# An expert's weight tile read as one run of 8192 bytes a partition instead of two of 4096

## The chip, the cores and the metric

The kernel runs on one core of one Trainium2 chip; the other cores are idle. The metric is the device time of one execution in microseconds (us), of which medians over several runs are given.

## The reference

Two transformer blocks one after the other, all in float32, over 256 tokens of 1024 channels. What matters here is the end of the second block, a mixture of 16 experts in which each expert chooses 32 of the 256 tokens:

```
aff  = softmax(h @ w_router)                        # 256 x 16
gate, idx = top_k(aff.T, 32)                        # every expert picks 32 tokens
xe   = h[idx]                                       # 16 x 32 x 1024
hid  = silu(xe @ w_gate[e]) * (xe @ w_up[e])        # w_gate, w_up: 16 x 1024 x 1024
ye   = (hid @ w_down[e]) * gate                     # w_down: 16 x 1024 x 1024
out  = scatter-add of ye at idx;  then x + g2 * out and a last rms norm
```

The three expert weights hold 16 x 3 x 4 MB = 201 MB, nearly half of the 427 MB that the kernel moves.

## The kernel before

All weights come through one DMA queue, that of SyncE (SP), as tiles of 1 MB: 128 partitions x 2048 floats. An expert takes 12 of them: slots 0 to 3 are its gate weight, 4 to 7 its up weight, 8 to 11 its down weight, and each tile holds 256 rows (input channels) of 1024 columns. `exp_tiles` cuts a weight so that partition p of tile j holds rows 256j + p and 256j + 128 + p, one behind the other; `expert_load` (line 536) issues the DMA.

The tiles go to 12 places (six in `ring`, six in `ahead`, a part of the arena) and, for the first three tiles of expert 1, to three buffers that are free by then (`extra`, in `gated` and `squares`). The first 15 tiles (expert 0's twelve and those three) are issued before the expert loop. The other 177 are `reused_load(u)`, u = 0 to 176, in the order in which PE uses them. Each waits (`slot_free`) until PE has multiplied the tile that lay in its place, twelve tiles earlier, the three extra ones not counted. So u = 0 waits for expert 0's first product, u = 12 for the fourth product of expert 1, and u = 21, the 22nd, for the first product of expert 2.

PE first gathers the chosen tokens by a product with a 0/1 matrix (`gather`, line 1136): 128 channels of `tok` are its stationary operand, and its output, channels on partitions, becomes `x_exp` and then `x_cur`. This is done for experts 0 to 3 before expert 0 (the early gather), for the others within expert 1 (`gather_others`). In `expert`, `product` (line 1156) multiplies one tile: for k = 0, 1 and two column halves, `src[:, 2 * j + k, :]` (32 columns) is stationary and a 512-column piece of the weight tile moves. After gate and up, ScalarE (ACT) and VectorE (DVE) make `hid_e`, PE turns it (line 1169, the hid turn: 128 columns of `hid_e` stationary) to `hid_t`, the four down products follow, and `y_e` is spread back over the tokens (line 1183). `product`, the gathers and the hid turn agree on which channel lies on which partition, since the rows of both operands are summed over partitions.

Of the kernel before, what the change touches and what calls it, by code (L numbers as in the profile page):

```python
# [19 lines left out]
P = 128  # L20
D = 1024
KD = D // P
# [151 lines left out]
def build(nc, x, positions, ffn_norm1, ffn1_w1, ffn1_w3, ffn1_w2, mix_norm, ffn_norm2, ffn2_w1, ffn2_w3, ffn2_w2,  # L174
# [15 lines left out]
    with ExitStack() as ctx:  # L190
# [10 lines left out]
        ps = ctx.enter_context(nc.psum_tensor("banks", [P, 8, 512], F32))  # L201
# [20 lines left out]
        tok = sb("tok", [P, TT, D])  # L222
# [29 lines left out]
        ident, ones = const("ident"), const("ones")  # L252
# [81 lines left out]
        picks = r4.take(2 * TT, EXPERTS, CAP)  # L334
        pick_cur, x_cur, spread_cur = r4.take(TT, CAP), r4.take(KD, CAP), r4.take(T)
        half_g, half_u, half_y, gate_act = r4.take(512), r4.take(512), r4.take(512), r4.take(512)
        gate_sum, up_sum, hid_e, y_e = r4.take(512), r4.take(512), r4.take(512), r4.take(512)
# [85 lines left out]
        def _(sp):  # L423
# [104 lines left out]
                cols(FIRST["branch"] + 2 + j, w_branch_b_2[0], 512 * j, 512, 4)  # L528
            for j in range(4):
                cols(FIRST["w_out"] + j, w_out_2[0], 256 * j, 256, KD)  # L530
            exp_tiles = [w[0].rearrange("e (j k p) c -> j e p k c", p=P, k=2)[j]
                         for w in (w_exp_gate_2, w_exp_up_2, w_exp_down_2) for j in range(4)]
            def expert_load(view, s, e, full, more=None):

                src = exp_tiles[s][e] if more is None else exp_tiles[s][e:][bass.ds(more, 1)].rearrange("o p k c -> p (o k) c")
                sp.dma_start(view.rearrange("p (k c) -> p k c", k=2), src).then_inc(full, 16)

            def first_load(s):
                expert_load(expert_view(s), s, 0, expert_full(s)[0])
# [30 lines left out]
            for i in range(2 * TT):  # L570
                t, g = i // 2, i % 2
# [7 lines left out]
        def _(pe):  # L579
            mm = pe.matmul  # L580
# [26 lines left out]
            for k in range(KD):  # L607
                for t in range(TT):
                    last = pe.transpose(ps[:, 2 + k // 2, (k % 2) * T + t * P:(k % 2) * T + t * P + P],
                                        tok[:, t, k * P:k * P + P], ident)  # L610
# [96 lines left out]
            for j in range(KD):  # L707
                n = FIRST["pw1"] + j
# [3 lines left out]
                if j == 0:  # L712
# [4 lines left out]
                    for k in range(KD):  # L717
                        last = pe.transpose(ps[:, 6, k * CONV_W:(k + 1) * CONV_W], rows_dw[:, k * P:k * P + P],
                                            ident[0:CONV_W, 0:CONV_W])
# [30 lines left out]
            for c in range(MOD_EARLY):  # L750
# [7 lines left out]
                if c == 2:  # L758
                    pe.wait_ge(sem("ctx_in"), 16)
                    pe.wait_ge(sem("glu_ready"), KD // 2)  # L760
                    for k in range(KD):
                        for t in range(TT):
                            last = pe.transpose(ps[:, k // 2, (k % 2) * T + t * P:(k % 2) * T + t * P + P],
                                                tok[:, t, k * P:k * P + P], ident)
# [17 lines left out]
            for j in range(4):  # L782
                n = FIRST["mla_a"] + j
                wait_full(pe, n)
                for o in range(2):
                    for k in range(KD):
                        if j == 0 and o == 0 and k % 2 == 0:
                            pe.wait_ge(sem("piece_normed"), NORM_PIECES["mla"] + k // 2 + 1)
                        if j < 3:
                            last = mm(ps[:, j, o * T:o * T + T], slot(n)[:, k * 256 + o * P:k * 256 + o * P + P],  # L790
                                      x_in[:, k, :], start=(k == 0), stop=(k == KD - 1))
                        else:
                            last = mm(ps[64 * o:64 * o + 64, j, 0:T], slot(n)[:, k * ROPE:k * ROPE + ROPE],
                                      x_in[:, k, :], start=(k == 0), stop=(k == KD - 1))
# [8 lines left out]
            for j in range(4):  # L803
                n = FIRST["uq"] + j
# [8 lines left out]
                for k in range(4):  # L813
                    for o in range(2):
                        c = k * 384 + 192 * o + NOPE
                        last = mm(ps[64 * o:64 * o + 64, b + 1, 0:T], slot(n)[:, c:c + ROPE], latent_n[:, k, :],
                                  start=(k == 0), stop=(k == 3))
# [3 lines left out]
            for j in range(2):  # L821
                n = FIRST["ukv"] + j
# [7 lines left out]
                for t in range(TT):  # L830
                    for k in range(2):
                        w = slot(n)[:, k * D:(k + 1) * D].rearrange("p (o c) -> p o c", o=4)[:, :, NOPE:NOPE + VH]
                        last = mm(ps[:, 2 + t, :], latent_n[:, 4 + k, t * P:t * P + P], w, start=(k == 0), stop=(k == 1))
                done(last)
            flat = rope_in.rearrange("p a t -> p (a t)")
            for c, (a, b) in enumerate(((0, 512), (512, 1024), (1024, 1280))):
                last = mm(ps[:, 5 + c, 0:b - a], const("rope_rot"), flat[:, a:b], start=True, stop=True)
# [128 lines left out]
            for dr in range(2):  # L966
                for s in range(TT):
                    for hd in range(HG_HEADS):
                        last = pe.transpose(ps[:, 2 * dr + s, hd * P:hd * P + P], key_dec[:, dr, hd, s * P:s * P + P], ident)
# [3 lines left out]
            for dr in range(2):  # L973
                for hd in range(HG_HEADS):
                    for s in range(TT):
                        last = mm(ps[:, 4 + dr, hd * P:hd * P + P], key_dec_t[:, dr, s, hd * P:hd * P + P],
                                  hg_v[:, s, hd * P:hd * P + P], start=(s == 0), stop=(s == TT - 1))
# [4 lines left out]
            for hd in range(HG_HEADS):  # L982
                o = ps[:, hd // 2, (hd % 2) * T:(hd % 2) * T + T]
                for s in range(TT):
                    mm(o, hg_v[:, TT + s, hd * P:hd * P + P], hg_p[:, s, hd, :], start=(s == 0), stop=False)
                for dr in range(2):
                    last = mm(o, state0[:, dr, hd, :], q_dec[:, dr, hd, :], start=False, stop=(dr == 1))
            last.then_inc(sem("pe_mark"), 1)
            pe.wait_ge(sem("hg_sq_ready"), 1)
            for c in range(2):  # L990
                last = mm(ps[:, 2 + c, :], ones[:, 0:P], o_sq[:, 2 * c:2 * c + 2, :].rearrange("p a t -> p (a t)"),
                          start=True, stop=True)
# [7 lines left out]
            for c in range(2):  # L1000
                last = mm(ps[:, 6 + c, :], const("headsum"), att_sq[:, 1024 + 512 * c:1536 + 512 * c], start=True, stop=True)
# [7 lines left out]
            for o in range(ATT_KV):  # L1009
                last = mm(ps[:, 6, o * T:o * T + T], const("axial_rot"), att_kr[:, o, T:2 * T], start=True, stop=True)  # L1010
# [50 lines left out]
            for br, src in ((0, o_hg), (1, o_att)):  # L1061
                if br == 1:
                    pe.wait_ge(sem("o_att_ready"), 1)
                for j in range(2):
                    n = FIRST["branch"] + 2 * br + j
# [3 lines left out]
                    for o in range(4):  # L1069
                        for k in range(4):  # L1070
                            last = mm(ps[:, 2 * j + o // 2, (o % 2) * T:(o % 2) * T + T],  # L1071
                                      slot(n)[:, k * 512 + o * P:k * 512 + o * P + P], src[:, k, :],
                                      start=(k == 0), stop=(k == 3))
# [5 lines left out]
            for k in range(KD):  # L1079
                last = mm(ps[32 * (k // 4):32 * (k // 4) + 32, 2, (k % 4) * P:(k % 4) * P + P],  # L1080
                          mod[:, 5 * KD + k, 0:1].to_broadcast([P, 32]), ident, start=True, stop=True)
            last.then_inc(sem("pe_mark"), 1)
            pe.wait_ge(sem("router_in"), 16)
            for t in range(TT):
                for k in range(KD):
                    if t == 0 and k % 2 == 0:
                        pe.wait_ge(sem("modulated"), SHIFTED["experts"] + k // 2 + 1)
                    last = mm(ps[:, 1, t * EXPERTS:(t + 1) * EXPERTS], x_in[:, k, t * P:t * P + P], router[:, k, :],
                              start=(k == 0), stop=(k == KD - 1))
# [11 lines left out]
            for t in range(TT):  # L1101
                last = pe.transpose(ps[0:EXPERTS, 0, t * P:t * P + P], aff[:, t, :], ident)
            last.then_inc(sem("pe_mark"), 1)
            for k in range(2, KD):
                last = rows(k)
# [18 lines left out]
            for t in range(TT):  # L1124
                last = pe.transpose(ps[:, 6, t * EXPERTS:(t + 1) * EXPERTS], slot_t[0:EXPERTS, t * P:t * P + P],
                                    ident[0:EXPERTS, 0:EXPERTS])
# [5 lines left out]
            def gather(k, bank, column, first, n):  # L1132

                o = ps[:, bank, column:column + n * CAP]
                for t in range(TT):
                    last = mm(o, tok[:, t, k * P:k * P + P], picks[:, t, first:first + n, :], start=(t == 0),  # L1136
                              stop=(t == TT - 1))
                return last

# [8 lines left out]
            def expert(more, e, take, early=False, gathers=False, final=False):  # L1148

                def product(m, j, src):  # L1150

                    w = take(4 * m + j)
                    for k in range(2):
                        for half in range(2):
                            g = 32 * (2 * k + half)
                            last = mm(ps[g:g + 32, 4 + m, :], src[:, 2 * j + k, :],  # L1156
                                      w[:, k * D + 512 * half:k * D + 512 * half + 512],
                                      start=(j == 0), stop=(j == 3))
                    done(last)

                pe.wait_ge(sem("x_cur_ready"), more + (e + 1))
                pe.wait_ge(sem("x_exp_taken"), 2 if early else 2 + KD)
                for m in range(2):
                    for j in range(4):
                        product(m, j, x_cur)
                pe.wait_ge(sem("hid_ready"), more + (e + 1))
                pe.wait_ge(sem("spread_cur_ready"), more + (e + 1))
                for c in range(4):
                    last = mm(ps[:, 7, 64 * c:64 * c + 64], hid_e[0:64, P * c:P * c + P], ident[0:64, 0:64],  # L1169
                              start=True, stop=True)  # L1170
                last.then_inc(sem("hid_turned"), 1)
                pe.wait_ge(sem("hid_t_ready"), more + (e + 1))
                for j in range(4):
                    if j == 2 and not final:
                        spread(more, e + 1)
                        if gathers:
                            gather_others()
                    product(2, j, hid_t)
                pe.wait_ge(sem("y_ready"), more + (e + 1))
                for t in range(TT):  # L1180
                    for half in range(2):
                        rows_ = slice(32 * half, 32 * half + 32)
                        last = mm(ps[:, 2 * t + half, :], spread_cur[rows_, t * P:t * P + P], y_e[rows_, :],
                                  start=False, stop=False, skip_group_check=True)
                    if final:
                        last.then_inc(sem("moe_out"), 1)
                if not final:
                    last.then_inc(sem("spread_free"), 1)
# [11 lines left out]
            for k in range(KD):  # L1200
                last = gather(k, 4 + k // 4, (k % 4) * P, 0, FIRST_EXPERTS)
# [1116 lines left out]
```

## Time and profile before

| | us |
|---|---|
| median of 3 runs | 1942.82 |
| lowest and highest | 1941.06, 1943.17 |
| span of the profiled execution | 1941.0 |

No separate time is given for the profiled execution; its span lies 0.1 us under the lowest of the three runs and 1.8 us under their median. In the views, PE is a matmul, PEld the load of its stationary operand, SPq the DMA issue on SyncE's queue. A "packet" is one contiguous run moved by one of the core's 16 DMA engines; besides the data, each transfer ends with one packet of 4 bytes on each engine, which counts under "under 512 B". The DMA share is the mean over the 16 engines; packets that overlap on an engine can push it over 100%.

### The profile page before, as it was taken

What the parts mean: (1) busy time and instruction counts of PE and PEld (TensorE: products, weight loads), DVE (VectorE), ACT (ScalarE), POOL (GpSimd) and SP (SyncE); (2) the same over time, 40 slices, a digit from 0 to 9 for tenths busy, and PEclk for the clock granted to TensorE, in tenths of its full rate; (3) what the DMA queues carried; (4) which work ended last, traced back from release to release, by engine and by line L of the source; (5) the groups of instructions that cost most, each with busy time, mean ns of one, the idle gap of its engine ahead of it and who ended that gap; (6) DMA issues with size and microseconds to landing.
All of it is one profiled execution on the core that took longest, in us unless ns stands there. A gap on an engine that the chain in (4) does not pass through costs nothing.

```text
span 1941.0 us, 28522 instructions
## 1 busy us (share of the span) xinstructions
PE 1744.2 (90%) x11819; PEld 1382.5 (71%) x11819; DVE 825.3 (43%) x1161; ACT 670.7 (35%) x957; POOL 10.7 (1%) x8
## 2 busy tenths in 40 slices
PE   6999998999999999999999999998998866766666
PEld 6999987999999998769999857786774321221211
DVE  4555697755565555134556405632322111101111
ACT  4444557643454343133434413325412211111111
POOL 0000010000000000000000000000000000000000
PEclk9999999999999999999999999999998977767777
DMA  9555455455545554525555632231276999999997
GB/s 305 186 173 194 152 185 184 131 195 173 194 152 192 176 190 132 175 94 163 192 186 174 197 105 87 87 119 55 82 308 270 409 410 410 410 410 410 410 410 313
DMA packets 223427, 427.08 MB, mean 220 GB/s; under 512 B 9139, under 2 KB 146661, under 8 KB 223364
## 3 DMA queue, kind: packets, MB, share of 16 engines
q1 hardware_dynamic: 223364, 426.18, 60.9%
q8 instruction: 46, 0.75, 0.2%
q14 instruction: 17, 0.14, 0.0%
HBM read 425.11 MB, written 1.05 MB: 220 GB/s over the span
## 4 chain that ended last, share of the span: by engine, by line
PE 78%; DMA 12%; DVE 5%; ACT 3%; SPq 1%; issue 1%; DVEq 0%; ACTq 0%
PE banks L596 14%; PE banks L597 14%; PE banks L598 14%; DMA ring<-in_w_exp_up 12%; PE banks L1156 7%; PE banks L946 4%; PE banks L922 3%; PE banks L698 3%; PE banks L746 2%; PE banks L1169 1%; PE banks L1071 1%; PE banks L927 1%; PE banks L623 1%; PE banks L790 1%; PE banks L908 1%; PE banks L1136 1%
## 5 line engine op out<-in xcount | busy, mean ns | idle before, releaser
L596 PE MATMUL banks<-x_split,w_split 128*128 128x256 f32 x1600 | 458.5, 287 | 19.2 <-DVE x_split L1743 9.7
L597 PE MATMUL banks<-x_split,w_split 128*128 128x256 f32 x1600 | 455.7, 285 | 0.0
L598 PE MATMUL banks<-x_split,w_split 128*128 128x256 f32 x1600 | 455.4, 285 | 0.0
L1726 DVE TENSOR_TENSOR w_split<-ring,w_split 128x1024 fp32r<-128x1024 f32 x288 | 346.7, 1225 | 248.6 <-ACT w_split L1259 248.2
L1259 ACT ACTIVATE w_split<-ring 128x1024 fp32r<-128x1024 f32 x288 | 296.1, 1051 | 200.4 <-PE banks L598 191.3
L596 PEld LDWEIGHTS banks<-x_split,w_split 128*128 128x128 f32 x1600 | 310.1, 194 | 22.9 <-issue 16.2
L597 PEld LDWEIGHTS banks<-x_split,w_split 128*128 128x128 f32 x1600 | 310.3, 194 | 0.1
L598 PEld LDWEIGHTS banks<-x_split,w_split 128*128 128x128 f32 x1600 | 310.1, 194 | 0.0
L596 PE MATMUL banks<-hid_split,w_split 128*128 128x256 f32 x704 | 199.6, 284 | 0.0
L597 PE MATMUL banks<-hid_split,w_split 128*128 128x256 f32 x704 | 199.2, 283 | 0.0
L598 PE MATMUL banks<-hid_split,w_split 128*128 128x256 f32 x704 | 199.2, 283 | 0.0
L1156 PE MATMUL banks<-ring,arena 128*32 128x512 f32 x768 | 130.0, 773 | 68.5 <-DMA ring<-in_w_exp_up 58.3
L596 PEld LDWEIGHTS banks<-hid_split,w_split 128*128 128x128 f32 x704 | 135.1, 192 | 0.7 <-DVE hid_split L1795 0.7
L598 PEld LDWEIGHTS banks<-hid_split,w_split 128*128 128x128 f32 x704 | 135.1, 192 | 0.0
L597 PEld LDWEIGHTS banks<-hid_split,w_split 128*128 128x128 f32 x704 | 135.1, 192 | 0.0
L1156 PE MATMUL banks<-arena 128*32 128x512 f32 x744 | 127.0, 800 | 0.6 <-ACT arena L1615 0.5
L1156 PEld LDWEIGHTS banks<-ring,arena 128*32 128x32 f32 x768 | 19.8, 120 | 149.0 <-DMA ring<-in_w_exp_up 111.8
L946 PE MATMUL banks<-xn,ring 128*128 128x256 f32 x448 | 99.4, 380 | 1.3 <-ACT arena L1508 0.7
L946 PEld LDWEIGHTS banks<-xn,ring 128*128 128x128 f32 x448 | 84.3, 190 | 13.9 <-issue 1.2
L1156 PEld LDWEIGHTS banks<-arena 128*32 128x32 f32 x744 | 32.4, 137 | 70.3 <-issue 63.2
L1296 ACT ACTIVATE hid_split<-gated 128x512 fp32r<-128x512 f32 x44 | 27.8, 632 | 152.2 <-DVE gated L1793 152.2
L1780 DVE TENSOR_TENSOR gated<-banks,rstd 128x512 f32<-128x512 f32 x88 | 60.4, 686 | 35.7 <-PE banks L598 35.6
(339 smaller groups left out, 1825.4 us busy)
## 6 DMA issues: line engine op xcount, KB each, us to landing
ring<-in_ffn_w SPq DMA_DIRECT2D x132, 1024.0 KB, 5.1
ring<-in_w_exp_up SPq DMA_DIRECT2D x62, 1024.0 KB, 18.4
arena<-in_w_exp_down SPq DMA_DIRECT2D x49, 1024.0 KB, 18.4
arena<-in_w_exp_gate SPq DMA_DIRECT2D x42, 1024.0 KB, 18.3
ring<-in_w_mod SPq DMA_DIRECT2D x24, 1024.0 KB, 5.1
ring<-in_w_in SPq DMA_DIRECT2D x21, 1024.0 KB, 5.1
ring<-in_w_exp_gate SPq DMA_DIRECT2D x19, 1024.0 KB, 18.0
ring<-in_w_exp_down SPq DMA_DIRECT2D x15, 1024.0 KB, 18.1
```

What stands on the lines that cost most here:

```text
L596: mm(out_, hi, moving(0), start=start, stop=False, **kw)
L597: mm(out_, hi, moving(1), start=False, stop=False, **kw)
L598: return mm(out_, lo, moving(0), start=False, stop=stop, **kw)
L698: last = mm(ps[:, bank0 + tile // 2, (tile % 2) * T:(tile % 2) * T + T], slot(n)[:, k * half_cols + o * P:k * half_cols + o * P + P], src[ ...
L746: mm(ps[:, b, c:c + T], diag[:, q % DIAGS, :], conv_in[:, j, w:w + T], start=(w == 0), stop=(w == CONV_W - 1)).then_inc(sem("diag_used"), 1)
L922: last = mm(ps[:, b + o, :], slot(n)[:, k * 256 + o * P:k * 256 + o * P + P], xn[:, k, :], start=(k == 0), stop=(k == KD - 1))
L946: last = mm(ps[:, b, o * T:o * T + T], slot(n)[:, k * 256 + o * P:k * 256 + o * P + P], x_in[:, k, :], start=(k == 0), stop=(k == KD - 1))
L1156: last = mm(ps[g:g + 32, 4 + m, :], src[:, 2 * j + k, :], w[:, k * D + 512 * half:k * D + 512 * half + 512], start=(j == 0), stop=(j == 3))
L1259: fn(half_part(n, o, 0), half_slot(n, o, columns), ACT.Copy).then_inc(sem("half_hi"), 1)
L1296: fn(hid_split[:, c % 2, 0, :, :], hidden[:, c % 2, :, :], ACT.Copy).then_inc(sem("hid_hi"), 1)
L1726: ins = dve.tensor_tensor(half_part(n, o, 1), half_slot(n, o, columns), half_part(n, o, 0).bitcast(F32), ALU.subtract)
L1780: return dve.tensor_tensor(dst, ps[:, bank + c % 2, :].rearrange("p (k t) -> p k t", t=T), scale, ALU.mult)
```

## The change

Partition p of tile j now takes rows 256j + 2p and 256j + 2p + 1, which are neighbours in memory, so its 2048 floats are one run of 8192 bytes. To match, the gather takes for channel block k every second of the 256 channels of its pair (even ones for k even, odd ones for k odd), and the hid turn does the same with the columns of `hid_e`. So the two stationary operands are read with a step of two floats (8 bytes) instead of one. `product`, the weight tiles' places, the waits and the counts of all instructions stay.

```diff
-            exp_tiles = [w[0].rearrange("e (j k p) c -> j e p k c", p=P, k=2)[j]
+            exp_tiles = [w[0].rearrange("e (j p k) c -> j e p (k c)", p=P, k=2)[j]
                          for w in (w_exp_gate_2, w_exp_up_2, w_exp_down_2) for j in range(4)]
             def expert_load(view, s, e, full, more=None):
 
-                src = exp_tiles[s][e] if more is None else exp_tiles[s][e:][bass.ds(more, 1)].rearrange("o p k c -> p (o k) c")
-                sp.dma_start(view.rearrange("p (k c) -> p k c", k=2), src).then_inc(full, 16)
+                src = exp_tiles[s][e] if more is None else exp_tiles[s][e:][bass.ds(more, 1)].rearrange("o p c -> p (o c)")
+                sp.dma_start(view, src).then_inc(full, 16)
...
                 for t in range(TT):
-                    last = mm(o, tok[:, t, k * P:k * P + P], picks[:, t, first:first + n, :], start=(t == 0),
+                    w = tok[:, t, :].rearrange("p (j c i) -> p j i c", j=KD // 2, i=2)[:, k // 2, k % 2, :]
+                    last = mm(o, w, picks[:, t, first:first + n, :], start=(t == 0),
                               stop=(t == TT - 1))
...
                 for c in range(4):
-                    last = mm(ps[:, 7, 64 * c:64 * c + 64], hid_e[0:64, P * c:P * c + P], ident[0:64, 0:64],
+                    w = hid_e[0:64, :].rearrange("p (j c i) -> p j i c", j=2, i=2)[:, c // 2, c % 2, :]
+                    last = mm(ps[:, 7, 64 * c:64 * c + 64], w, ident[0:64, 0:64],
                               start=True, stop=True)
```

## Rows read from the trace of the kernel before

**Rows 1.** The page: span, PE clock, DMA share and rate in 40 slices.
```profile
span 1941.0 us, 28522 instructions
PEclk9999999999999999999999999999998977767777
DMA  9555455455545554525555632231276999999997
GB/s 305 186 173 194 152 185 184 131 195 173 194 152 192 176 190 132 175 94 163 192 186 174 197 105 87 87 119 55 82 308 270 409 410 410 410 410 410 410 410 313
```

**Rows 2.** Engine table by stretches: busy us, PE clock, DMA share, GB/s.
```profile
1470.00:1561.00 91.00, 73.31 (x510) 27.96 (x508) 12.29 (x18) 20.00 (x42) 0.00 (x0) 0.91 0.99 393
1561.00:1930.00 369.00, 250.83 (x1440) 74.27 (x1432) 40.95 (x60) 43.03 (x94) 0.00 (x0) 0.73 1.02 406
```

**Rows 3.** Chain of work that ended last, in time (start, us, what).
```profile
1464.38 5.48 PE banks L1136 x32
...
1592.98 18.38 DMA ring<-in_w_exp_up
1611.41 1.98 PE banks L1156 x8
...
1622.67 19.41 DMA ring<-in_w_exp_up
1642.13 1.98 PE banks L1156 x8
...
1918.61 1.98 PE banks L1156 x8
```

**Rows 4.** Timeline of PEld at the last expert's down products.
```profile
1925.13 0.20 PEld L1156 LDWEIGHTS banks<-ring,arena 128*32 128x32 f32 x8 [0.66 <-ACT arena L1615]
...
1928.55 0.20 PEld L1156 LDWEIGHTS banks<-arena 128*32 128x32 f32 x4 [0.66 <-issue]
1929.08 0.12 PEld L1156 LDWEIGHTS banks<-arena 128*32 128x32 f32 x4 [0.34 <-DMA arena<-in_w_exp_down]
```

**Rows 5.** DMA in 1650 to 1850: all packets; then packets, MB, share.
```profile
DMA packets 21255, 81.92 MB, mean 410 GB/s; under 512 B 1257, under 2 KB 1257, under 8 KB 21255
q1 hardware_dynamic: 21255, 81.92, 102.6%
```

**Rows 6.** DMA in 1107.5 to 1121.5, tiles of `in_w_in` in runs of 1024 bytes.
```profile
DMA packets 4887, 4.93 MB, mean 352 GB/s; under 512 B 68, under 2 KB 4887, under 8 KB 4887
q1 hardware_dynamic: 4887, 4.93, 109.5%
```

**Rows 7.** DMA in 3 to 4, the load of `consts`, runs of 6284 bytes.
```profile
DMA packets 63, 0.40 MB, mean 396 GB/s; under 512 B 0, under 2 KB 0, under 8 KB 63
q1 hardware_dynamic: 63, 0.40, 97.7%
```

**Rows 8.** Timeline of SyncE's queue, 1472 to 1530.
```profile
1472.10 0.37 SPq L536 DMA_DIRECT2D ring<-in_w_exp_gate  x1
1472.96 2.94 SPq L536 DMA_DIRECT2D ring<-in_w_exp_up  x4
1476.39 0.37 SPq L536 DMA_DIRECT2D ring<-in_w_exp_down  x1
1477.25 6.88 SPq L536 DMA_DIRECT2D arena<-in_w_exp_down  x3
1485.35 3.88 SPq L536 DMA_DIRECT2D arena<-in_w_exp_gate  x3
1497.06 0.38 SPq L536 DMA_DIRECT2D ring<-in_w_exp_gate  x1
1497.91 5.67 SPq L536 DMA_DIRECT2D ring<-in_w_exp_up  x4
1505.13 0.85 SPq L536 DMA_DIRECT2D ring<-in_w_exp_down  x1
1506.15 13.80 SPq L536 DMA_DIRECT2D arena<-in_w_exp_down  x3
1525.09 2.70 SPq L536 DMA_DIRECT2D arena<-in_w_exp_gate  x3
```

**Rows 9.** DMA rate in 40 slices of 0.1 us, 1471 to 1475.
```profile
GB/s 0 0 0 0 0 164 0 0 0 0 0 0 0 0 0 0 0 0 0 0 0 328 287 41 0 0 0 0 0 205 410 369 492 451 369 451 451 369 451 369
```

**Rows 10.** Line 1136, 1460 to 1475: ns min/median/max, first and last start.
```profile
L1136 PEld LDWEIGHTS banks<-arena,tok x32: 186/262/333, 1464.4 to 1469.5; 128*128 128x128 f32 x32
```

**Rows 11.** DMA issues by line: count, KB, us to landing.
```profile
arena<-in_w_exp_down SPq DMA_DIRECT2D x49, 1024.0 KB, 18.4
```

## The prediction

> **What bounds the kernel now.** I read the page first [rows 1]. From slice 31 on, the last 430 us, the DMA engines are full at 409 or 410 GB/s while PE's granted clock falls to seven tenths. The engine table says the same by stretch [rows 2]: from 1561 to 1930, PE is busy for 251 of 369 us and the DMA share is 1.02. The chain of waits gives the rhythm [rows 3]: PE starts on the last up tile of one expert at 1611.41 and of the next at 1642.13, 30.72 us apart, and the longest piece between is the transfer. An expert is 12 tiles, so a tile takes 30.72 / 12 = 2.560 us, that is 1.0486 MB at 409.6 GB/s. There the kernel's time is tiles times 2.560 us.
>
> How far back does this reach? The first of the 177 reused tiles is issued at 1472.10 [rows 8], and the rate rises at 1473.9, the slices being 0.1 us [rows 9]: 1.8 us from issue to data. 173 tiles later it is 1473.9 + 173 x 2.560 = 1916.8, and PE starts on the last up tile, the 173rd, at 1918.6 [rows 3]; the 1.8 us between are the way from the last byte to PE. So the DMA engines never run dry in between, although PE, not DMA, is late until about 1561. The four down tiles behind the last up tile follow at 2.560 us, and PE waits for the last of them, at 1929.08 [rows 4]. But PE had begun the part before it at 1928.55 and is at most 0.3 us early: the way through the hid turn and three down tiles is as long as the four transfers. A faster DMA gains nothing on these four, so 173 tiles count.
>
> **What a tile costs, now and after.** I take a tile's time as packets of one engine times a fixed cost f, plus the bytes' own time B. Two long stretches with a full queue give both.
> - 4096-byte runs: 16 packets and the closing one, 17 on each engine; 2.560 us. The stretch has 81.92 MB in 21255 packets, 1257 of them closing ones, so 19998 runs of 4096 bytes [rows 5].
> - 1024-byte runs: 64 + 1 = 65 packets; 4.93 MB are 4.70 tiles, in 14 us: 2.978 us [rows 6].
>
> 48 packets more cost 0.418 us: f = 8.7 ns, and B = 2.560 - 17 x 0.0087 = 2.412 us. After the change an engine has 8 + 1 = 9 packets a tile: 2.412 + 9 x 0.0087 = **2.490 us**, 0.070 less. That needs a run of 8192 bytes to go as one packet. The load of `consts` has runs of 6284 bytes and shows 0.40 MB in 63 packets, so a run over 4096 bytes isn't cut there [rows 7].
>
> The same row gives the other end. Those packets take 0.977 x 16 x 1 us / 63 = 248.1 ns, where the model says 8.7 + 6284 x 2412 / 65536 = 240.0. If the 8.1 ns more are the price of 2188 bytes beyond 4096, 4096 bytes beyond cost 15.2 ns, and the tile takes 2.490 + 8 x 0.0152 = 2.612 us, 0.052 more than now. The sign hangs on this. I take 2.490: the `consts` rows lie 6284 bytes apart, so they start at uneven addresses, and they move in the kernel's first 4 us; the new runs start at multiples of 8192 bytes and stand in a queue that is long full, as the 4096-byte ones do.
>
> Transfers: 173 x 0.070 = **-12.1 us**.
>
> The Trainium skill (DMA: Bandwidth & Descriptors, § Why small descriptors are slow) gives a packet some 3 cycles of fixed cost, 3.5 ns at the 850 MHz that it names, where the trace leaves 8.7. By it the transfers would win 8 x 3.5 = 28 ns a tile, 4.9 us in all, and joining packets of this size would not be worth while.
>
> **A gap that opens.** The queue stays full only if PE frees places in time. The tightest point is expert 2's start: 1+4+1+3+3+1+4+1+3 = 21 tiles are issued in the groups up to that of 1506.15, and the 22nd only at 1525.09, when PE has multiplied expert 2's first tile [rows 8]. Its data can flow at 1525.09 + 1.8 = 1526.9. The 21 tiles end now at 1473.9 + 21 x 2.560 = 1527.7: covered, by 0.8 us. After, they end at 1473.9 + 21 x 2.490 = 1526.2, and PE's way to that point has no wait for DMA and does not move: the engines stand still for 0.7 us. Behind it places come free at some 1.2 us each (2.70 us for three issues [rows 8]), faster than they are filled. **+0.7 us**, once.
>
> **The stationary operands with a step of two.** The early gather lies on the chain, 32 loads and matmuls in 5.48 us [rows 3], and both expert 0 and the first reused tile wait for it. Its loads take 186 to 333 ns [rows 10]. I know no load in the trace with a step, so I bound the cost by 0 and by the widest spread of a 128-column load, 333 - 186 = 147 ns: 32 x 0.147 = 4.7 us in the gather and 8 x 0.147 = 1.2 us in the last hid turn, 5.9 us in all. The turns before that end while DMA is waited for, and the second gather's loads lie under matmuls of 384 columns. Below 0 it isn't: as many columns are read as before. I take 0, because number and width of the reads stay; both ends stay for the range.
>
> The Trainium skill (SBUF — State Buffer, § Door 1: The DMA port swizzle) charges steps by lines of 16 bytes and wants two hits or more in each; with 8 bytes there are exactly two. No run here shows it; by it the term is 0 as well.
>
> **Covered.** The first 15 tiles are loaded long before PE wants them; what they gain is lost in that wait. If they came at the old pace nothing would change. Of tiles in flight there are 18.4 / 2.56 = 7 [rows 11]; should that be a limit of packets, more fit in, and SyncE waits for PE's free places where it now stands at the issue. The engines have work either way.
>
> Sum: -12.1 + 0.7 + 0 = **-11.4 us**. The span becomes 1941.0 - 11.4 = 1929.6. The median of the runs lies 1.8 us above that span; against it the forecast is 1942.8 - 11.4 = **1931.4 us**, 0.59% less.
>
> **Rivals.**
> - *The steps cost.* The loads slow down and the chain grows by up to 5.9 us: 1931.4 + 5.9 = 1937.3. For it: no row excludes it. Against it: it takes the whole spread of the trace. 8%.
> - *The run is cut* into two packets of 4096 bytes, and nothing changes: 1942.8. For it: no run of 8192 bytes is in this queue now. Against it: 6284 bytes went whole [rows 7]. 6%. The Trainium skill (DMA: Bandwidth & Descriptors, § SWDGE vs HWDGE vs iDMA) has packets of preferably 4096 bytes at most; the 6284-byte packets do not keep to that.
> - *Long packets are slower a byte (the slower side).* With 2.612 us a tile: 173 x 0.052 = +9.0, so 1951.8. It decides from (2560 - 9) / 8 = 319 ns a packet, where mine takes 310. For it: [rows 7] as they stand. Against it: uneven addresses, the kernel's start. 6%.
> - *f belongs to the short runs.* The 1024-byte runs lie far apart in memory, and part of their 8.7 ns may be that and not the packet. With half of it saved a tile, the transfers win 6.0 us, no gap opens to speak of, and the time is 1936.8. For it: one pair of sizes is all that f rests on. 5%.
>
> **How the numbers follow.** My forecast has 75%. Its own range is 1928 to 1935: 2 ns more or less on a packet move 8 x 0.002 x 173 = 2.8 us, and the gap and PE's clock in the last expert may add 1 us. A measurement of this kernel tells about 0.2%, 3.9 us, from no change. Faster by more than that: forecast, steps and half of f, less a little for their edge near 1938.9: 0.86. Within: the cut run and that edge, 0.08. Slower: 0.06. The range, 1927 to 1939, takes in the steps and half of f and leaves out the cut run and the slow packets, 12%.
>
> **What the profile after would show.** In the steady stretch the closing packets rise a little, the others halve to 128 a tile (cut run: unchanged). The rhythm of the last up tiles is 12 x 2.490 = 29.9 us and the rate 421 GB/s (half of f: 415; slow packets: 401). Line 1136's piece still takes 5.5 us (steps cost: up to 10.2). A dip in the DMA rate stands near 1526. The last up tile is multiplied at 1907.2, and the span ends 22.4 us behind it, as now. If the rhythm is right and the span isn't, the loss stands before 1474 or behind that tile. I would be wrong altogether if memory could not give 421 GB/s for 450 us, which nothing in this trace asks of it.

## The result and the profile after

The changed kernel takes 1930.8 us (median of 4 runs, 1928.6 to 1934.7) against 1943.0 for the kernel before on the same chips: ratio 0.9940, interval 0.9928 to 0.9951, so 10 to 14 us less. The forecast was 1931.4. The profiled execution was the fastest of the four: its span of 1926.8 us lies 4.0 us under the median, where the span before lay 1.8 under, so times are compared by medians and ratios, and spans only to find the places.

The page of the kernel after, for [rows 1]: span, PE clock, DMA share and rate in 40 slices.

```profile
span 1926.8 us, 28517 instructions
PEclk9999999899999999999999999999998978778777
DMA  9555456355546554534555552321185999999997
GB/s 302 193 174 188 161 176 197 119 188 194 176 153 197 177 190 139 163 121 134 194 190 180 161 166 66 110 88 65 66 314 233 421 422 422 422 422 422 422 422 315
```

The stretch that is bound by transfers stands where it stood, at 422 GB/s instead of 410. The DMA view of 1650 to 1850, for [rows 5], all packets and then packets, MB and share:

```profile
DMA packets 11596, 84.41 MB, mean 422 GB/s; under 512 B 1293, under 2 KB 1293, under 8 KB 1293
q1 hardware_dynamic: 11596, 84.41, 101.3%
```

11596 - 1293 = 10303 packets carry 84.41 MB: 8192 bytes each, none between 512 B and 8 KB. So a run of 8192 bytes goes whole. A tile takes 1.0486 MB / 422.05 GB/s = 2.485 us, 75 ns less than the 2.560 before; the forecast was 2.490.

The chain of the kernel after at the early gather and at the last up tile, for [rows 3], and SyncE's queue around expert 2, for [rows 8]:

```profile
1464.16 4.05 PE banks L1137 x32
...
1904.20 1.98 PE banks L1157 x8
```

```profile
1470.46 0.33 SPq L536 DMA_DIRECT2D ring<-in_w_exp_gate  x1
...
1522.52 2.04 SPq L536 DMA_DIRECT2D arena<-in_w_exp_gate  x3
```

The spans differ by 1941.0 - 1926.8 = 14.2 us, and these rows place them. The first reused tile is issued at 1470.46 instead of 1472.10: 1.6 us, most of it from the early gather, which takes 4.05 us in this profile instead of 5.48. From that issue to the last up tile it is 433.7 us instead of 446.5: 12.8. Behind the last up tile it is 22.6 us instead of 22.4: 0.2 given back. 1.6 + 12.8 - 0.2 = 14.2.

Two readings need an experiment each. The 12.8 us should be fewer packets, but the new runs also make each tile one unbroken megabyte of memory. And the gather got shorter although its loads now have a step.

### The profile page after: what moved, and what is told of

It is laid out like the page before. It is cut to its first block, busy times and chain, and to the rows that moved or that the text cites. A ratio compares the mean times of both kernels' runs of the same rounds, so it can differ in the third digit from the quotient of the medians.

```text
span 1926.8 us, 28517 instructions
## 1 busy us (share of the span) xinstructions
PE 1735.9 (90%) x11814; PEld 1379.8 (72%) x11819; DVE 825.4 (43%) x1161; ACT 670.7 (35%) x957; POOL 10.7 (1%) x8
## 4 chain that ended last, share of the span: by engine, by line
PE 77%; DMA 10%; DVE 5%; SPq 4%; ACT 3%; issue 1%; DVEq 0%; ACTq 0%
PE banks L596 14%; PE banks L597 14%; PE banks L598 14%; DMA ring<-in_w_exp_up 10%; PE banks L1157 6%; PE banks L946 4%; PE banks L922 3%; SPq L536 3%; PE banks L698 3%; PE banks L746 2%; PE banks L1071 1%; PE banks L927 1%; PE banks L623 1%; PE banks L790 1%; PE banks L1185 1%
## 5 line engine op out<-in xcount | busy, mean ns | idle before, releaser
L1157 PE MATMUL banks<-ring,arena 128*32 128x512 f32 x768 | 126.5, 756 | 62.4 <-DMA ring<-in_w_exp_up 52.2
L1157 PE MATMUL banks<-arena 128*32 128x512 f32 x744 | 120.5, 761 | 0.5 <-ACT arena L1617 0.5
## 6 DMA issues: line engine op xcount, KB each, us to landing
arena<-in_w_exp_down SPq DMA_DIRECT2D x49, 1024.0 KB, 25.5
```

Source lines behind the costliest of these rows:

```text
L1157: last = mm(ps[g:g + 32, 4 + m, :], src[:, 2 * j + k, :], w[:, k * D + 512 * half:k * D + 512 * half + 512], start=(j == 0), stop=(j == 3))
```

## The experiments

Each ran beside the kernel before on the same chip. The changed kernel has medians of 1930.8 and, further below, 1934.2 us, so ratios to the kernel before are compared, and a difference in us is told by ratio unless medians are named.

**One part alone.** `dma_only` keeps the new tiles and drops the steps; `step_only` keeps the steps and drops the new tiles.

```diff
# dma_only, against the changed kernel
-                    w = tok[:, t, :].rearrange("p (j c i) -> p j i c", j=KD // 2, i=2)[:, k // 2, k % 2, :]
+                    w = tok[:, t, k * P:k * P + P]
...
-                    w = hid_e[0:64, :].rearrange("p (j c i) -> p j i c", j=2, i=2)[:, c // 2, c % 2, :]
+                    w = hid_e[0:64, P * c:P * c + P]
# step_only, against the changed kernel
-            exp_tiles = [w[0].rearrange("e (j p k) c -> j e p (k c)", p=P, k=2)[j]
+            exp_tiles = [w[0].rearrange("e (j k p) c -> j e p k c", p=P, k=2)[j]
```

> The 8192-byte runs alone: both stationary operands (gather, hid turn) are read without a step again, so channels and weight rows no longer match and the output is not the reference's; transfers and instruction counts are those of the changed kernel. Theory (the whole gain is the transfers'): 2.485 us a tile as in the changed kernel, time 1930.8 within 2 us. Rival (the step of two costs something on the way that is not hidden): faster than the changed kernel, by up to 5.9 us, 1925 to 1929, and line 1137's loads at 190 ns instead of 196.

> The steps of two alone: the weight tiles come in two runs of 4096 bytes as before, so the output is not the reference's. Theory: the steps are free where they stand, 1943.0 within 2 us, 2.560 us a tile, the loads of the late gather at 196 ns instead of 190. Rival (steps cost on the chain): up to 1948.9.

`dma_only`: 1930.0 us, ratio 0.9935 (0.9922 to 0.9949), the same as the changed kernel's within the intervals. `step_only`: 1943.9 us, ratio 1.0000 (0.9991 to 1.0009). The whole gain is the transfers', and the steps of two cost nothing that can be measured in the kernel's time. What they do to a load shows in the late gather, line 1137 in 1500 to 1520, where the granted clock is high (mean 0.94 in 1500 to 1530 in both; ns min/median/max; first the changed kernel, then `dma_only`):

```profile
L1137 PEld LDWEIGHTS banks<-arena,tok x32: 195/196/332, 1504.3 to 1514.5; 128*128 128x128 f32 x32
```

```profile
L1137 PEld LDWEIGHTS banks<-arena,tok x32: 190/190/338, 1503.5 to 1513.9; 128*128 128x128 f32 x32
```

6 ns a load, 0.2 us for 32 of them. The early gather says the same where the clock is high throughout: 4.05 us with the step (the changed kernel, `step_only`), 3.85 without (`dma_only`, and `pad` and `late_before` below).

**The same memory in two packets.** `cut` takes the same neighbouring rows but writes the second one first, so that the run can't be one packet; the product reads the halves the other way round.

```diff
# cut, against the changed kernel
-            exp_tiles = [w[0].rearrange("e (j p k) c -> j e p (k c)", p=P, k=2)[j]
+            exp_tiles = [w[0].rearrange("e (j p k) c -> j e p k c", p=P, k=2)[j]
...
-                sp.dma_start(view, src).then_inc(full, 16)
+                sp.dma_start(view.rearrange("p (k c) -> p k c", k=2)[:, ::-1, :], src).then_inc(full, 16)
...
-                                      w[:, k * D + 512 * half:k * D + 512 * half + 512],
+                                      w[:, (1 - k) * D + 512 * half:(1 - k) * D + 512 * half + 512],
```

> Partition p still takes the neighbouring rows 2p and 2p + 1 of a tile, but writes row 2p + 1 first and 2p second, which makes it two packets of 4096 bytes over the same 8192 bytes of memory; the product reads the halves in that order. Theory (a fixed cost for each packet, 17 a tile on each engine): 2.560 us a tile as before, 1943 within 2 us. Rival (the gain comes from neighbouring rows, memory read in one stretch of 1 MB, not from fewer packets): 2.485 us a tile and 1931.

1943.2 us, ratio 1.0001 (0.9992 to 1.0010), and in 1650 to 1850:

```profile
q1 hardware_dynamic: 21248, 81.92, 102.6%
```

But for 7 packets these are the packets, the bytes and the share of the kernel before [rows 5], over the memory order of the changed one. Neighbouring rows as such give nothing; fewer packets give all.

**More packets.** `runs2048` cuts the tiles of the kernel before into runs of 2048 bytes.

```diff
# runs2048, against the kernel before
-            exp_tiles = [w[0].rearrange("e (j k p) c -> j e p k c", p=P, k=2)[j]
+            exp_tiles = [w[0].rearrange("e (j k p) (h c) -> j e p h k c", p=P, k=2, h=2)[j]
...
-                                      w[:, k * D + 512 * half:k * D + 512 * half + 512],
+                                      w[:, (2 * half + k) * 512:(2 * half + k) * 512 + 512],
```

> The kernel before with its tiles cut into runs of 2048 bytes: 33 packets a tile on each engine. Theory (8.7 ns for each packet whatever its length): 2.412 + 33 x 0.0087 = 2.699 us a tile, 173 x 0.139 = 24 us more, 1967 within 3 us. Rival (the fixed cost read from 1024-byte runs belongs mostly to those short runs, half of it here): 2.63 us a tile, 12 us more, 1955.

1971.9 us, ratio 1.0144 (1.0129 to 1.0158), 28 us more, a little beyond the band that was expected, and in 1650 to 1850:

```profile
DMA packets 38957, 77.37 MB, mean 387 GB/s; under 512 B 1181, under 2 KB 1181, under 8 KB 38957
```

77.37 MB in 200 us is 2.710 us a tile. So 9, 17 and 33 packets a tile on each engine take 2.485, 2.560 and 2.710 us: 75 ns for 8 packets and 150 ns for 16, 9.4 ns a packet both times. The straight line holds, a little steeper than the 8.7 of the forecast, and the rival, half of f, is out. The packets one by one agree: in these stretches the traces give data packets of 2048, 4096 and 8192 bytes mean durations of 88.5, 163.5 and 313.6 ns, so twice the bytes cost less than twice the time.

**Longer runs, and longer steps.** `wide` loads two tiles as one transfer of four neighbouring rows a partition; the 12 places become six of double size, and one pair instead of three tiles goes to the extra buffers. `step8` is the kernel before with steps of 8 floats in the gathers and 4 in the hid turn, and no other change.

```diff
# wide, against the changed kernel
-            exp_tiles = [w[0].rearrange("e (j p k) c -> j e p (k c)", p=P, k=2)[j]
-                         for w in (w_exp_gate_2, w_exp_up_2, w_exp_down_2) for j in range(4)]
+            exp_tiles = [w[0].rearrange("e (j p k) c -> j e p (k c)", p=P, k=4)[j]
+                         for w in (w_exp_gate_2, w_exp_up_2, w_exp_down_2) for j in range(2)]
...
-                    w = tok[:, t, :].rearrange("p (j c i) -> p j i c", j=KD // 2, i=2)[:, k // 2, k % 2, :]
+                    w = tok[:, t, :].rearrange("p (j c i) -> p j i c", j=KD // 4, i=4)[:, k // 4, k % 4, :]
...
-                    w = take(4 * m + j)
+                    w = take(2 * m + j // 2)[:, (j % 2) * SLOT:(j % 2) * SLOT + SLOT]
# step8, against the kernel before
-                    last = mm(o, tok[:, t, k * P:k * P + P], picks[:, t, first:first + n, :], start=(t == 0),
+                    w = tok[:, t, :].rearrange("p (c i) -> p i c", i=8)[:, k, :]
+                    last = mm(o, w, picks[:, t, first:first + n, :], start=(t == 0),
```

> Two tiles as one transfer: a partition takes four neighbouring rows, one run of 16384 bytes, the 12 places become 6 of double size, one extra place instead of three, and gather and hid turn read with a step of four floats. Theory (T = B + n f with f = 9.4 ns and B = 2.400 us for 1 MB, from 2.485, 2.560 and 2.710 us for 9, 17 and 33 packets): two tiles take 4.800 + 9 x 0.0094 = 4.885 us, 2.442 each, 173 x 0.043 = 7.4 us less than the changed kernel, of which the end gives 0.9 back, where two tiles land together: 1924.3 within 2.5 us. Rivals: fewer places in flight open gaps, or a run of 16384 bytes is cut or slower a byte (no gain, 1930.8); the step of four, one float of a 16-byte line, slows the loads of the gather from 196 to 300 ns or more (up to 5 us on the chain, 1929).

> The changed kernel once more, beside the wide one on the same chip. Both theories: 1930.8 within 2 us and 2.485 us a tile. Its profile shows a second time how long the early gather takes (4.05 us in the first profile, 5.48 before): if PE's clock decides that, it varies with no change of the code.

> The kernel before with its gathers reading every eighth channel (a step of 32 bytes) and the hid turn every fourth column; the rows no longer match, so the output is not the reference's. Theory (a load's time depends on the lines of 16 bytes that it touches): line 1137's loads well over 196 ns, 300 to 800. Rival (any step costs the same few ns, as the 6 ns of the step of two): 196 to 200 ns and the time of before.

On one chip `wide` took 1933.8 us, ratio 0.9949 (0.9935 to 0.9962), and `again`, the changed kernel, 1934.2, ratio 0.9953 (0.9939 to 0.9966): no difference. The tile itself did nearly what the theory says. The wide kernel in 1650 to 1850:

```profile
DMA packets 5886, 85.69 MB, mean 428 GB/s; under 512 B 656, under 2 KB 656, under 8 KB 656
```

85.69 MB in 200 us is 2.447 us a tile, where 2.442 was expected: 173 x 0.037 = 6.4 us less than the changed kernel. They were lost elsewhere, and the 1924.3 that was expected did not come. The early gather, line 1138 of `wide` and then line 1137 of `step8`, in 1460 to 1475:

```profile
L1138 PEld LDWEIGHTS banks<-arena,tok x32: 308/330/330, 1463.5 to 1470.7; 128*128 128x128 f32 x32
```

```profile
L1137 PEld LDWEIGHTS banks<-arena,tok x32: 312/336/337, 1464.0 to 1471.4; 128*128 128x128 f32 x32
```

These loads take at least 308 ns, where loads with steps of 1 and 2 go down to 186 and 193, and the clock is not why: it was 1.00 all through both gathers. The gather takes 7.75 and 7.93 us, 2 us more than the longest seen without such a step. The hid turn takes 2.08 us in both, against 1.10 before and 1.15 with a step of two, and it comes twice before expert 2. The Trainium skill (SBUF — State Buffer, § Door 1: The DMA port swizzle) has lines of 16 bytes and wants two hits or more in each; a step of 8 bytes has two, steps of 16 and 32 bytes have one. The trace agrees: the step of 8 bytes costs 6 ns a load, those of 16 and 32 bytes both cost some 120 ns.

`step8`, a single run, took 1949.2 us against 1943.5 for the kernel before, with its tiles at the old 410 GB/s. Its profile has the rest of the way: the gather is 2.4 us longer, and the rate in 1515 to 1555 lacks 3.3 us against 410 GB/s, in the place that the next experiments are about. `wide` lost its gain in two ways. It issues its first pair at 1474.36, 4 us after the changed kernel's first tile, and the gap in the same place costs it 3.0 us, where the changed kernel loses 0 to 1.8.

`again` also answers the question on the gather. The same code took 5.58 us here and 4.05 in the first profile:

```profile
1462.58 5.58 PE banks L1137 x32
```

The kernel before took 5.48, and `dma_only`, `step_only` and `pad` took 3.85, 4.05 and 3.85. What differs is PE's granted clock. In 1466 to 1468 (the clock is the third number from the end), the kernel before and then the first profile of the changed one:

```profile
1466.00:1468.00 2.00, 2.00 (x11) 2.00 (x11) 0.00 (x0) 0.00 (x0) 0.00 (x0) 0.51 0.00 0
```

```profile
1466.00:1468.00 2.00, 2.00 (x19) 2.00 (x18) 0.00 (x0) 0.60 (x1) 0.00 (x0) 1.00 0.00 0
```

0.51 is the lower of the clock's two levels, 1.2 GHz, and 1.00 the upper, 2.4 GHz. So the 1.4 us at the gather are not the change. Nor does a long gather alone make a late start: `again` reached its gather at 1462.58, 1.6 us sooner than the first profile did, and issued its first reused tile at 1470.40, as that one did. With the old tiles and no steps the first issue stands at 1472.10 before, but at 1470.65 in `pad` and 1470.30 in `late_before`.

**The gap.** The second profile of the changed kernel shows what the first did not. SyncE's queue, and the rate in 1515 to 1555, a slice a microsecond:

```profile
1523.54 2.69 SPq L536 DMA_DIRECT2D arena<-in_w_exp_gate  x3
```

```profile
GB/s 442 401 401 418 426 434 401 426 410 213 319 426 320 205 336 377 418 426 442 418 418 442 426 401 434 418 442 410 442 410 418 426 418 434 418 426 410 442 401 426
```

From 1524 to 1531 the rate falls as low as 205: against 422, the six low slices lack (209 + 103 + 102 + 217 + 86 + 45) / 422 = 1.8 us. From the first issue to the last up tile this profile takes 436.5 us, 2.7 more than the first, so only 10.0 less than before. The 22nd tile was issued 53.1 us behind the first one here and 52.1 us behind it in the first profile; at 2.485 us a tile the engines need it by 52.2. In the kernel before the distance was 53.0, and 21 x 2.560 = 53.8 would have done. `step_only`, at the old pace, had 55.4 and lost 1.7 us in the same place: 1.6 by this count. In `again` the count gives 53.1 - 52.2 = 0.9 us, about the first of its two dips; what makes the second, when the next tiles have been issued, stays open.

How late the 22nd tile comes goes with the clock that PE is granted in 1470 to 1500. The first profile, `again` and `step_only`:

```profile
1470.00:1500.00 30.00, 23.06 (x187) 7.86 (x179) 5.46 (x8) 6.88 (x13) 0.00 (x0) 0.94 0.96 394
```

```profile
1470.00:1500.00 30.00, 23.92 (x180) 7.51 (x172) 4.70 (x7) 6.87 (x13) 0.00 (x0) 0.89 0.96 392
```

```profile
1470.00:1500.00 30.00, 25.16 (x176) 8.06 (x168) 4.09 (x6) 6.13 (x11) 0.00 (x0) 0.83 0.98 386
```

At 0.94 the distance is 51.6 to 52.1 us (`pad`, `dma_only`, the first profile), at 0.89 it is 53.0 to 53.2 (before, `again`, `cut`), at 0.83 it is 55.4. So PE's clock in experts 0 and 1 decides on this gap, and a faster tile makes it more likely. `late_after` and `late_before` bring PE there earlier, by cutting the late gather to eight small products.

```diff
# late_after against the changed kernel, late_before against the kernel before
-                    gather(k, 4 + k % 2, 0, FIRST_EXPERTS, EXPERTS - FIRST_EXPERTS).then_inc(sem("x_exp_product"), 1)
+                    mm(ps[:, 4 + k % 2, 0:CAP], tok[:, 0, k * P:k * P + P], picks[:, 0, 4, :], start=True,
+                       stop=True).then_inc(sem("x_exp_product"), 1)
```

> The changed kernel with the late gather, 32 loads and matmuls of 384 columns in expert 1, cut to one small product for each of its eight blocks, so that experts 4 to 15 work on wrong tokens; transfers and waits stay. Theory (the gap near 1526 is PE's lateness at expert 2's first product): that product comes 8 us earlier, the DMA rate has no dip, 0 to 2 us less than the changed kernel's median. Rival (the dip seen in the second profile is of the DMA engines' own making): it stays.

> The same cut in the kernel before. Theory (its engines are full from 1474 to 1927, PE's late gather costs nothing): the time of before within 1.5 us. Rival (PE's work in expert 1 is on the path before too): up to 8 us less.

`late_after`: 1928.1 us, ratio 0.9916 (0.9903 to 0.9930), against 0.9940 and 0.9953 for the changed kernel; the spread of its runs shrank to 1927.9 to 1930.7. The rate in 1515 to 1555 has no dip:

```profile
GB/s 426 434 410 418 418 426 426 418 426 426 434 401 426 418 426 426 418 426 426 434 410 418 410 426 434 410 426 426 434 418 418 410 426 434 410 426 426 426 410 426
```

`late_before`: 1941.2 us, ratio 0.9986 (0.9977 to 0.9995). The theory allowed 1.5 us, and it was 2.7. It would fit that the kernel before has this gap too in some of its runs, as `step_only` had, but that is not shown: its profile has none, and from the first issue to the last up tile `late_before` takes 446.6 us, as the kernel before does (446.5). `late_after` is 5 and 7 us under the changed kernel by the two ratios, more than a gap of 0 to 1.8 us gives; each interval is 5 us wide, and whether anything else is in it stays open. In these two the 22nd tile is issued 49.9 and 48.4 us behind the first, 2 to 5 us sooner and not 8.

The pair gives one more reading. Both ran on one chip, both without the late gather and without a gap: 1941.2 - 1928.1 = 13.1 us, and 173 tiles at 0.0755 us less are 13.1 us.

**The best version.** `wide_turned` takes the steps of four away: the copy into `tok` and the product that makes `hid_e` write their columns in the order in which they are loaded. `wide_late` also moves the late gather behind expert 1's last down product, where it runs beside the making of y.

```diff
# wide_turned, against wide
-            fn(tok[:, :, :].rearrange("p t d -> p (t d)"), banks(4, 4), ACT.Copy).then_inc(sem("rows_copied"), 1)
+            fn(tok[:, :, :].rearrange("p t (j i c) -> p (t j) c i", j=2, i=4), banks(4, 4).rearrange("p (a c i) -> p a c i", a=4, i=4),
+               ACT.Copy).then_inc(sem("rows_copied"), 1)
...
# wide_late, against wide_turned
                         spread(more, e + 1)
-                        if gathers:
-                            gather_others()
                     product(2, j, hid_t)
+                if gathers:
+                    gather_others()
```

> The wide kernel (16384-byte runs, 9 packets for two tiles), with the order of channels made where data is copied anyway: the copy into tok and the product that makes hid_e write their columns sorted by channel modulo 4, so that gather and hid turn load without a step. Theory (the wide kernel lost its gain to the loads with a step of four, 7.75 us for the early gather instead of 4.1 to 5.6, and to a gap behind them near 1530): the early gather is back at 4 to 5.6 us, the tile stays at 2.444 us, 3 to 5 us less than the wide kernel's 1933.8: 1929 to 1931. Rival (half as many places of double size are what opens the gap): the DMA rate still falls near 1530 and the time stays within 2 us of 1933.8.

> The wide kernel with sorted copies, and the late gather moved behind expert 1's last down product, so that it runs while ScalarE and VectorE make y of expert 1 (their copies of its output follow y's). All outputs as before. Theory (PE's lateness at expert 2's first product opens the gap, 2.3 us in the profile of the kernel without the move): that product comes 3 to 4 us sooner, the gap shrinks to under 1 us, and the time falls from 1929.5 to 1926 to 1928. Rival (the gap comes from having six double places, whatever PE does): the gap and the time stay.

`wide_turned`: 1929.5 us, ratio 0.9917 (0.9903 to 0.9930), the early gather at 5.48 us, the tile at 2.446. That settles the steps of four: taken away, they give back 4 us of the median and 6 by the ratio. `wide_late`: 1926.1 us, ratio 0.9915 (0.9902 to 0.9929). SyncE's queue near the tile pair that needs expert 2's products, first `wide_turned`, then `wide_late`:

```profile
1527.08 2.06 SPq L538 DMA_DIRECT2D ring<-in_w_exp_gate  x2
```

```profile
1524.11 2.06 SPq L538 DMA_DIRECT2D ring<-in_w_exp_gate  x2
```

The move does what it was meant to, 3.0 us earlier, and the rate in 1515 to 1555 stays between 393 and 475 GB/s. But there was little left to win. The rate of `wide_turned` in 1515 to 1555 shows no gap of 2.3 us as expected; against 429 GB/s its 40 slices lack 0.3 us in all:

```profile
GB/s 426 442 426 426 442 442 393 442 410 426 426 426 426 393 360 410 442 393 426 492 360 459 459 360 475 393 393 475 426 410 475 393 442 475 377 426 492 344 459 442
```

The pair was issued 54.1 us behind the first, and 22 x 2.446 = 53.8 would have done; in `wide` it was 57.0. In ratio the two are not apart. Both beat the kernel before by 16 us, and by ratio they are 4 to 7 us under the two measurements of the changed kernel (the interval of the nearer one, 0.9928 to 0.9951, just meets theirs). Their profiles, 1927.7 and 1926.3 us, are no shorter than the 1926.8 of the changed kernel's first: the shorter tile is paid for by a later first issue, at 1472.96 and 1473.83 instead of 1470.46. Part of that is the pair, which waits for two products; part is the clock before and in the gather.

**An open one.** `pad` tests why the `consts` packets were slow, with rows of 6400 bytes.

```diff
+    parts["pad"] = np.zeros((P, -at % 64))
```

> The kernel before with rows of 6400 bytes in the constants (zeros at the end) instead of 6284, so that each starts at a multiple of 256 bytes. Theory (the 248 ns of the 6284-byte packets were their uneven addresses): 9.4 + 6400 x 2400 / 65536 = 243.8 ns a packet in the window of 3 to 4 us. Rival (the kernel's start makes them slow, whatever their address): 252 ns or more.

In 3 to 4, and with a time of 1940.9 us (one run):

```profile
q1 hardware_dynamic: 65, 0.42, 102.0%
```

1.020 x 16 x 1 us / 65 = 251.1 ns, 7 over the theory and 1 under the rival. It leans to the start of the kernel and not the address, but 65 packets don't decide it. That neither touches long runs in a full queue is shown by the changed kernel.

## Why the prediction was right

- **The bound and the count of tiles.** 173 tiles times what one saves is 173 x 0.0755 = 13.1 us, and 12.8 were seen between the first issue and the last up tile. The last four gain nothing: behind the last up tile the span is 0.2 us longer, and PE, no longer DMA, is what the last down tile waits for. In [rows 4] it was DMA; now the load at that place starts after 0.58 us of plain issue:

```profile
1914.91 0.12 PEld L1157 LDWEIGHTS banks<-arena 128*32 128x32 f32 x4 [0.58 <-issue]
```

This hangs on the clock of that stretch, 0.54 and 0.52 in the 11 us behind the last up tile. In `late_before` and `pad`, both with the old tiles, it was 0.69 and 0.78, and PE waited 1.4 and 1.5 us for DMA at the last down tile; there a faster tile would have gained something.
- **The price of a packet.** The mechanism was right and its size a little off: f is 9.4 ns, not 8.7, so a tile takes 2.485 us and not 2.490, and the transfers give 13.1 us and not 12.1. The 8.7 rested on tiles of 65 packets from another weight, whose time lies 33 ns under the new line. The slope of the `consts` rows, the other bound, had the wrong sign.
- **The 3 cycles a packet of the Trainium skill** (DMA: Bandwidth & Descriptors, § Why small descriptors are slow). The estimate from them was 28 ns a tile, and the same section calls joining descriptors worth it only up to 256 bytes. Here 75 ns were saved, by joining runs of 4096 bytes. The measurement decides.
- **The gap.** Forecast at 0.7 us, it is absent in the first profile and 1.8 us in the second. The place was right. A step that failed is "PE's way to that point has no wait for DMA and does not move": with PE's clock it moves, from 51.6 to 55.4 us between profiles of kernels that do the same work there, and that is more than the reserve.
- **The steps.** Taken as 0, they are 0.2 us in the gather. The upper bound of the forecast, 147 ns, was the spread of loads at two clocks and no measure of steps; that a step of four or more costs about as much (120 ns) is chance.
- **The start.** 1.6 us of the profile's 14.2 lie before the first issue. They belong to neither kernel: with the old tiles `pad` and `late_before` issue as early. That PE's clock sets them is shown for the gather and argued for the rest.
- **The sum.** The medians lie 12.2 us apart on the first measurement and 9.3 on the second (1943.5 and 1934.2), and the forecast of 11.4 between them. Direction and mechanism are borne out; that the first median came within 0.6 us was in part luck, since the term of the transfers was 1.0 us too small, and gap and clock move single runs by more than that.

## What to carry to other kernels

Where the DMA engines are full, count the packets of a tile as well as its bytes: here 9.4 ns each whatever their length from 2048 to 8192 bytes, so rows that lie side by side in memory should go to one partition, and whatever is multiplied with them takes the same order. Make that order where data is copied or computed anyway; a stationary operand may be read with a step of two floats, not of four. And before a transfer-bound stretch is made faster, look for the place at its start where the queue's reserve is smallest: here it was under 1 us, less than what PE's clock varies by.

## What the runs showed that was not expected

- A run of 16384 bytes a partition also goes as one packet (5230 data packets for 85.69 MB), and the cost per packet is only a little lower: 4.5 packets fewer a tile save 37 ns, 8.2 each.
- Loads of 128 float columns at the high clock: 186 to 192 ns without a step, 193 to 198 with a step of two, 307 to 330 with a step of four, and hardly more, 312 to 337, with a step of eight (single loads of 332 to 338 ns in late gathers left out). At the lower clock a load without a step takes up to 333.
- Time from issue to landing rose from 18.4 us [rows 11] to 25.5, from 7 tiles in flight to 10, with half the packets, and fell to 14.4 with twice as many. It is neither a fixed number of tiles nor of packets (7.2 x 17 = 122, 5.3 x 33 = 175 an engine); what sets it stays open, and no time was seen to hang on it.
